# A four-layer decoder trunk on one core: who makes the remainders of layer 2's weights

## The chip, the cores and the metric

One core of one Trainium2 chip runs the whole program in one launch. The metric is the device time of an execution in microseconds; lower is better. The engines are TensorE (PE, matmuls), VectorE (DVE), ScalarE (ACT), GpSimd (POOL) and SyncE (SP, which issues DMAs). Their instruction streams run side by side and meet only at semaphores.

## The reference, cut to what matters

The input is x of 256 tokens by 2048 features in float32. Four pre-norm residual layers follow, whose mixers are differential attention, sliding-window attention with sinks, mLSTM, and differential attention again, and a final RMSNorm. Layer 2, the one that the change touches, is the sliding-window layer:

```python
proj = h @ w_in                     # h: 256 x 2048, w_in: 2048 x 4608
q, k, v, g = jnp.split(proj, [SW_WIDTH, SW_WIDTH + nkv, SW_WIDTH + 2 * nkv], axis=-1)
q = rope(q.reshape(B, S, SW_Q_HEADS, d), cos, sin) * (d ** -0.5)
...
o = o.reshape(B, S, SW_WIDTH) * jax.nn.silu(g.astype(jnp.float32))
return o.astype(h.dtype) @ w_out    # w_out: 2048 x 2048
```

It has 32 query heads and 4 key/value heads of width 64.

## The kernel before, in words

**Three products for one.** Each float32 operand of a projection is split in two: a rounded part ("hi") and the remainder ("lo"). A product is then the sum of three matmuls: hi by hi, lo of the activations by hi of the weights, hi of the activations by lo of the weights (`three`, lines 1134 to 1138). The weights are split while they stream in.

**Jobs and pairs.** A projection is cut into jobs of 512 output columns. A job has 2048 rows of weights, 16 chunks of 128, worked in 8 pairs of chunks. A pair is a tile of 128 partitions by 1024 columns (512 KB). For each pair:

- SP loads `raw` (8 pairs of room, lines 640 to 653), when the pair eight before is done;
- ACT rounds it into `w_hi` (a ring of 4 pairs, lines 1065 to 1074) after waiting for the load and for the pair four before to be done, and raises `hi_ready`;
- DVE subtracts, `w_lo = raw - w_hi` (8 pairs of room, lines 2008 to 2016), after waiting for `hi_ready`, and raises `lo_ready`;
- PE waits for `lo_ready` (line 1317), makes 12 matmuls of 512 columns (2 chunks, 2 halves of the tokens, 3 products) and raises `pairs_done`.

There are 73 jobs, so 584 pairs. Layer 2 has one head job (keys and values), then four iterations of two jobs (512 columns of queries, 512 columns of the gate), then four jobs of the output projection. One iteration is thus 16 pairs, numbered 0 to 15 below, and serves 8 query heads.

**Side work.** Everything that isn't a projection is hung on pairs. `walk` (line 273) calls the function `pair` of every engine for the same pairs in the same order, and each of them first or last calls the layer's side function. A table written out by hand (`SW`, line 70) says at which pair each step is due; steps with a number of 16 or more fall in the next iteration. In layer 2, on DVE ahead of a pair's subtraction: the rope of the queries at pairs 11 and 12 (lines 1560 to 1565), sums of attention outputs (line 1727), the gating of the iteration before (line 1792), its split (line 1796, at pairs 13 and 14), the staging of the values (line 1744, at pair 15), and the lower half of the split of the queries (line 1759, from pair 15). On PE behind a pair's matmuls: the transposes of the queries at pair 11 (line 1102), and the scores of one head after each of the pairs 12 to 15 and the following four (lines 1209 to 1211). The scores of the first head wait for `split_lo`, which line 1759's first instruction raises; those of the second for the bank that its second instruction frees.

**GpSimd** does small things only: constants at the start, and the inverse roots of the norms (lines 724 to 731), three instructions on a handful of columns each time. In layer 2 it makes the layer's norm and then goes straight on to wait for the next layer's (line 742).

Of the kernel before, what the change touches and what calls it, by code (L numbers as in the profile page):

```python
# [22 lines left out]
F32 = mybir.dt.float32  # L23
F32R = mybir.dt.float32r
I32 = mybir.dt.int32
ALU = mybir.AluOpType
# [8 lines left out]
PAIRS = KC // 2  # L35
RING = 8
LAG = 4
ITERS = 4
# [5 lines left out]
LAYERS = [("da", 0), ("sw", 0), ("ml", 0), ("da", 1)]  # L44
NL = len(LAYERS)
HEAD_JOBS = {"da": 0, "sw": 1, "ml": 0}
ITER_JOBS = {"da": 4, "sw": 2, "ml": 4}
# [115 lines left out]
def in_iter(l, name, i, n):  # L163
    head, per, _ = _counts(l, name)
    return i * per + (BASE[name][l] + head + n)
# [7 lines left out]
def _jobs():  # L173

    first, loop, out, by = [], [], [], []
    for kind, _ in LAYERS:
        first.append(len(by))
        by += ["act"] * HEAD_JOBS[kind]
        loop.append(len(by))

        by += ITER_EMPTIED_BY[kind] * ITERS
        out.append(len(by))
        by += ["dve"] * OUT_JOBS
    return first, loop, out, by


JOB0, LOOP0, OUT0, EMPTIED_BY = _jobs()
# [82 lines left out]
        return (l, places.index(at)) if at in places else None  # L270


def walk(eng, l, pair, own=None, who=None):

    kind = LAYERS[l][0]
    nj = ITER_JOBS[kind]
    for p in range(PAIRS * HEAD_JOBS[kind]):
        pair(Place(l, "head", None, p), JOB0[l], 0, 0, p)
    for j in range(nj):
        for p in range(PAIRS):  # L280
            pair(Place(l, "iter", 0, j * PAIRS + p), LOOP0[l] + j, 0, j, p)
    with eng.Fori(1, ITERS) as i:
        if own:
            own.enter(i, OWN_STEPS[who, kind])
        for j in range(nj):
            for p in range(PAIRS):
                pair(Place(l, "iter", i, j * PAIRS + p), LOOP0[l] + j, i, j, p)
        if own:
            own.leave()
    for j in range(OUT_JOBS):  # L290
        for p in range(PAIRS):
            pair(Place(l, "out", None, j * PAIRS + p), OUT0[l] + j, 0, j, p)


def build(nc, x, positions, norm_g, final_g, da_w_in, da_w_out, da_lambda, da_subln_g, sw_w_in, sw_w_out,
          sw_sinks, ml_w_in, ml_b_gates, ml_w_out, ml_norm_g, freqs, out):
    ctx = ExitStack()
    with ctx:
        def sb(name, shape, dt=F32):
            return ctx.enter_context(nc.sbuf_tensor(name, shape, dt))  # L300

        def sem(name):
            return ctx.enter_context(nc.semaphore(name))
# [6 lines left out]
        with ExitStack() as place:  # L310
            raw = place.enter_context(nc.sbuf_tensor("raw", [P, KC, JW], F32))
        w_lo = sb("w_lo", [P, KC, JW], F32R)
        w_hi = sb("w_hi", [P, RING, JW], F32R)
# [172 lines left out]
        raw_full = [sem(f"raw_full{s}") for s in range(PAIRS)]  # L486
        raw_half = [sem(f"raw_half{s}") for s in range(PAIRS)]
        hi_ready, lo_ready = sem("hi_ready"), sem("lo_ready")
        first_in, first_hi, first_lo = sem("first_in"), sem("first_hi"), sem("first_lo")
        pairs_done = sem("pairs_done")  # L490
        act_emptied, dve_emptied = sem("act_emptied"), sem("dve_emptied")
# [205 lines left out]
        @block.gpsimd  # L697
        def _(pool):
            own = Own(pool, pool_own)

            def select(ap, compare, fill, base, step, channel):
                pool.affine_select(out=ap, in_=ap, compare_op=compare, fill=fill, base=base,
                                   pattern=[[step, P]], channel_multiplier=channel).then_inc(consts, 1)

            own.step(pool.memset(ident[:], 0.0))
            own.wait()
            select(ident[:], ALU.not_equal, 1.0, 0, -1, 1)
            for t in (masks, mask_ml, x_ss):
                own.step(pool.memset(t[:], 0.0))
            for t in (ones, tri):  # L710
                own.step(pool.memset(t[:], 1.0))
            own.step(pool.memset(half_pow[:], -0.5))
            own.step(pool.memset(eps_t[:], EPS))
            for width, t in inv_width.items():
                own.step(pool.memset(t[:], 1.0 / width))
            own.wait()

            for c in (1, 3):
                select(masks[:, P * c:P * c + P], ALU.is_ge, NEG, 0, -1, 1)
            select(masks[:, 2 * P:3 * P], ALU.is_gt, NEG, 0, 1, -1)  # L720
            select(mask_ml[:], ALU.is_ge, -NEG, 0, 1, -1)
            select(tri[:], ALU.is_ge, 0.0, 0, 1, -1)

            def inverse_root(to, ms, ss, width):

                n = ms.shape[1]
                own.step(pool.tensor_tensor(ms, ss, inv_width[width][:, 0:n], ALU.mult))  # L727
                own.wait()
                own.step(pool.tensor_tensor(ms, ms, eps_t[:, 0:n], ALU.add))
                own.wait()  # L730
                return pool.tensor_tensor(to, ms, half_pow[:, 0:n], ALU.pow)

            for l in range(NL):
                pool.wait_ge(x_summed, l + 1)
                inverse_root(rstd[:], x_ms[:], x_sum[:], D).then_inc(rstd_ready, 1)
                pool.wait_ge(rstd_ready, 2 * l + 1)
                pool.tensor_scalar(rstd_half[:], rstd[:], 0.5, 0.0, ALU.mult, ALU.add).then_inc(rstd_ready, 1)
                if l == 0:
                    wg_rows = ml_w_in[0, :, 3 * D:3 * D + 16].rearrange("(k p) n -> p k n", p=P)
                    pool.dma_start(wg_raw[:], wg_rows).then_inc(wg_in, 16)  # L740
                if LAYERS[l][0] == "sw":
                    continue
                kind = LAYERS[l][0]
                with pool.Fori(0, ITERS) as i:
                    own.more = i * OWN_STEPS["pool", kind]
                    if kind == "da":
                        for h in range(2):
                            pool.wait_ge(sig["ssq_done"], in_iter(l, "ssq_done", i, 2 * h + 2))
                            inverse_root(o_rs[:, h, :], o_ms[:, h, :], o_ss[:, h, :], S).then_inc(sig["o_rstd"], 1)
                    else:  # L750
                        flat = [a[:].rearrange("p a b -> p (a b)") for a in (o_rs, o_ms, o_ss)]
                        pool.wait_ge(sig["ssq_done"], in_iter(l, "ssq_done", i, 4))
                        inverse_root(*flat, S).then_inc(sig["o_rstd"], 1)
                own.more = 0
                own.n += (ITERS - 1) * OWN_STEPS["pool", kind]
            for t in range(T):
                pool.wait_ge(x_summed, NL + t + 1)
                pool.tensor_tensor(rstd[:, t:t + 1], x_ms[:, t:t + 1], half_pow[:, 0:1], ALU.pow).then_inc(rstd_ready, 1)
# [335 lines left out]
        def _(pe):  # L1094
# [216 lines left out]
            def pair(w, j0, i, j, p):  # L1311
                J = j0 + ITER_JOBS[w.kind] * i
                w.first_job_of_layer = j0 == JOB0[w.l] and (w.phase == "head" or w.first)
                if w.start and w.idx == 0:
                    pe.wait_ge(first_lo, 1)
                else:
                    pe.wait_ge(lo_ready, PAIRS * J + p + 1)
                slot, whole = 2 * (p % LAG), 2 * p
                if w.phase == "out":
                    j, p = OUT[w.kind]["order"][w.idx]  # L1320
                    j0 = OUT0[w.l] + j
# [45 lines left out]
                if w.start and w.idx in (0, 1, 3):  # L1367
                    n = {0: 1, 1: 2, 3: 3}[w.idx]
# [18 lines left out]
        def _(dve):  # L1387
# [605 lines left out]
            def pair(w, j0, i, j, p):  # L1993
                J = j0 + ITER_JOBS[w.kind] * i
                if (ln := w.x_due("sum")) is not None:
                    add_residual(*ln)
                if (ln := w.x_due("total")) is not None:
                    sum_squares(ln[0])
                if (ln := w.x_due("split")) is not None:
                    x_turned_lo(*ln)  # L2000
                if (ln := w.x_due("gain")) is not None and ln[0] == NL - 1:
                    final_gain(ln[1])
                sides[w.kind](w, w.l)
                if w.start and w.idx == 0:
                    dve.wait_ge(first_hi, 1)
                    dve.tensor_tensor(w_lo[:, 0, :], raw[:, 0, :], w_hi[:, 0, :].bitcast(F32), ALU.subtract)\
                       .then_inc(first_lo, 1)
                dve.wait_ge(hi_ready, PAIRS * J + p + 1)
                q = 2 * (p % LAG)
                if w.start and w.idx == 0:  # L2010
                    dve.tensor_tensor(w_lo[:, 1, :], raw[:, 1, :], w_hi[:, 1, :].bitcast(F32), ALU.subtract)\
                       .then_inc(lo_ready, 1)
                else:
                    two = slice(2 * p, 2 * p + 2)
                    dve.tensor_tensor(w_lo[:, two, :], raw[:, two, :], w_hi[:, q:q + 2, :].bitcast(F32),  # L2015
                                      ALU.subtract).then_inc(lo_ready, 1)
                if w.start:
                    start_up(w.idx)

# [3 lines left out]
            last = OUT_JOBS - 1  # L2023
# [62 lines left out]
```

## Time and profile before

| what | value |
| --- | --- |
| median of 3 runs | 1712.66 us (1712.31 to 1713.44) |
| the profiled execution's own time | 1712.57 us |
| its span, from the first to the last instruction | 1710.8 us |
| granted TensorE clock over the span | 0.999 of full speed |
| busy: PE, DVE, ACT, POOL | 1699.6, 1188.9, 911.4, 38.9 us |
| HBM traffic | 213 GB/s over the span |
| share of PE in the chain that ended last | 95% |

Busy times count an engine's own instructions, not its waits, branches or the issuing of DMAs. Ends of matmuls are modelled and matmuls overlap, so PE's lines are best read by their starts. A line's busy time is followed by the mean of one instruction in ns. Times in rows of a timeline are from the start of the span.

### The profile page before, as it was taken

What the parts mean: (1) busy time and instruction counts of PE and PEld (TensorE: products, weight loads), DVE (VectorE), ACT (ScalarE), POOL (GpSimd) and SP (SyncE); (2) the same over time, 40 slices, a digit from 0 to 9 for tenths busy, and PEclk for the clock granted to TensorE, in tenths of its full rate; (3) what the DMA queues carried; (4) which work ended last, traced back from release to release, by engine and by line L of the source; (5) the groups of instructions that cost most, each with busy time, mean ns of one, the idle gap of its engine ahead of it and who ended that gap; (6) DMA issues with size and microseconds to landing.
All of it is one profiled execution on the core that took longest, in us unless ns stands there. A gap on an engine that the chain in (4) does not pass through costs nothing.

```text
span 1710.8 us, 24445 instructions
## 1 busy us (share of the span) xinstructions
PE 1699.6 (99%) x7890; PEld 1417.7 (83%) x7890; DVE 1188.9 (69%) x1909; ACT 911.4 (53%) x1400; POOL 38.9 (2%) x99
## 2 busy tenths in 40 slices
PE   9999999999999999999999999999999999999998
PEld 7888888888888888888888888888888888888887
DVE  7767677775769888865656465656676676777756
ACT  7454555554656666655544545454554555455543
POOL 1000000000000000000000000000000000000000
PEclk9999999999999999999999999999999999999999
DMA  8768676766875555478998699966877686767673
GB/s 286 244 194 262 201 245 215 233 216 220 264 216 161 160 159 153 154 234 194 190 166 271 177 201 182 265 182 216 260 227 237 195 265 200 247 214 232 223 237 126
DMA packets 230035, 364.53 MB, mean 213 GB/s; under 512 B 14950, under 2 KB 80044, under 8 KB 229836
## 3 DMA queue, kind: packets, MB, share of 16 engines
q1 hardware_dynamic: 229536, 362.94, 73.5%
q8 instruction: 39, 0.64, 0.2%
q0 software_dynamic: 48, 0.13, 0.1%
q10 hardware_dynamic: 380, 0.56, 0.1%
q14 instruction: 32, 0.26, 0.0%
HBM read 335.79 MB, written 27.79 MB: 213 GB/s over the span
## 4 chain that ended last, share of the span: by engine, by line
PE 95%; DMA 2%; issue 1%; SPq 1%; DVE 1%; ACT 0%; DVEq 0%; POOLq 0%; POOL 0%; ACTq 0%
PE acc L1136 29%; PE acc L1137 29%; PE acc L1138 29%; PE tp L1102 1%; PE tp L1137 1%; PE tp L1136 1%; PE tp L1138 1%; DMA raw<-in_ml_w_in_dram 1%; PE sc L1137 1%; PE sc L1136 1%; PE sc L1138 1%; DMA xres<-in_x_dram 0%; DMA qs<-q_turning 0%; DMA q_turning<-scr 0%; PE sc L1162 0%
## 5 line engine op out<-in xcount | busy, mean ns | idle before, releaser
L2015 DVE TENSOR_TENSOR w_lo<-raw,w_hi 128x1024 fp32r<-128x1024 f32 x583 | 703.2, 1220 | 401.4 <-ACT w_hi L1074 399.0
L1074 ACT ACTIVATE w_hi<-raw 128x1024 fp32r<-128x1024 f32 x583 | 610.2, 1056 | 454.9 <-PE acc L1138 401.6
L1136 PE MATMUL acc<-w_hi,xt_hi 128*128 128x512 f32 x1824 | 715.3, 392 | 1.7 <-DVE w_lo L2015 1.0
L1138 PE MATMUL acc<-w_hi,xt_lo 128*128 128x512 f32 x1824 | 711.0, 390 | 0.0
L1137 PE MATMUL acc<-w_lo,xt_hi 128*128 128x512 f32 x1824 | 710.4, 389 | 0.0
L1138 PEld LDWEIGHTS acc<-w_hi,xt_lo 128*128 128x128 f32 x1824 | 342.4, 188 | 72.3
L1136 PEld LDWEIGHTS acc<-w_hi,xt_hi 128*128 128x128 f32 x1824 | 342.6, 188 | 70.3 <-DVE w_lo L2015 1.6
L1137 PEld LDWEIGHTS acc<-w_lo,xt_hi 128*128 128x128 f32 x1824 | 342.6, 188 | 67.3
L1136 PE MATMUL acc<-w_hi,ot_hi 128*128 128x512 f32 (+1 forms) x456 | 176.6, 387 | 0.0
L1138 PE MATMUL acc<-w_hi,ot_lo 128*128 128x512 f32 (+1 forms) x456 | 175.8, 386 | 0.0
L1137 PE MATMUL acc<-w_lo,ot_hi 128*128 128x512 f32 (+1 forms) x456 | 175.8, 385 | 0.0
L877 ACT ACTIVATE scr<-scr,neg_max_t 128x128 f32<-128x128 f32 (+1 forms) x128 | 57.3, 448 | 95.8 <-DVE neg_max_t L1591 75.6
L1138 PEld LDWEIGHTS acc<-w_hi,ot_lo 128*128 128x128 f32 x456 | 85.7, 188 | 17.2
L1136 PEld LDWEIGHTS acc<-w_hi,ot_hi 128*128 128x128 f32 x456 | 85.7, 188 | 16.8
L1137 PEld LDWEIGHTS acc<-w_lo,ot_hi 128*128 128x128 f32 x456 | 85.7, 188 | 16.7
L805 ACT ACTIVATE junk_x<-xres 128x512 f32<-128x512 f32 x38 | 24.0, 632 | 40.7 <-DVE xres L1980 40.1
L890 ACT ACTIVATE junk_o<-sc 128x256 f32<-128x256 f32 x32 | 12.3, 384 | 37.4 <-PE sc L1138 36.9
L727 POOL TENSOR_TENSOR o_ms<-o_ss,inv 128x2 f32<-128x2 f32 (+1 forms) x20 | 3.9, 197 | 1059.4 <-ACT junk_o L890 1059.4
L863 ACT ACTIVATE th<-acc,rstd_half 128x512 f32<-128x512 f32 x32 | 20.2, 682 | 12.8 <-PE acc L1138 12.8
L845 ACT ACTIVATE qs<-acc,rstd 128x512 f32<-128x512 f32 x32 | 20.3, 684 | 12.3 <-PE acc L1138 12.2
L1636 DVE SCALAR_TENSOR_TENSOR v_lo<-acc,rstd,v_hi 128x512 fp32r<-128x512 f32 x24 | 16.9, 746 | 13.6 <-ACT v_hi L855 13.6
L1136 PE MATMUL tp<-w_hi,ot_hi 128*128 128x512 f32 x64 | 24.9, 389 | 0.0
(306 smaller groups left out, 1226.5 us busy)
## 6 DMA issues: line engine op xcount, KB each, us to landing
raw<-in_da_w_in_dram SPq DMA_DIRECT2D x255, 512.0 KB, 4.4
raw<-in_ml_w_in_dram SPq DMA_DIRECT2D x96, 512.0 KB, 5.7
raw<-in_sw_w_in_dram SPq DMA_DIRECT2D x72, 512.0 KB, 3.7
raw<-in_da_w_out_dram SPq DMA_DIRECT2D x64, 512.0 KB, 4.0
raw<-in_sw_w_out_dram SPq DMA_DIRECT2D x32, 512.0 KB, 3.7
raw<-in_ml_w_in_dram SPq DMA_DIRECT2D x64, 256.0 KB, 7.3
raw<-in_ml_w_out_dram SPq DMA_DIRECT2D x32, 512.0 KB, 3.9
qs<-q_turning SPq DMA_DIRECT2D x12, 512.0 KB, 6.9
```

The costliest lines, as they stand in the source:

```text
L805: act.activation(junk_x[:], xres[:, t, JW * n:JW * n + JW], ACT.Square, accum_out=x_ss[:, t, n:n + 1]).then_inc(sig["x_sq"], 1)
L845: act.activation(dst[:, t], src, ACT.Copy, scale=rstd[:, t:t + 1]).then_inc(act_emptied, 1)
L863: act.activation(dst[:, t, :], acc[b][t][:], ACT.Tanh, scale=rstd_half[:, t:t + 1])\
L877: act.activation(scr[:, slot, cols], scr[:, slot, cols], ACT.Exp, bias=neg_max_t[:, slot, t:t + 1], scale=scale, accum_out=exp_sum[:, slot ...
L890: act.activation(junk_o[:], ml_values(h, t)[:, 0:S] if ml else sc[h][:, S * t:S * t + S], ACT.Square, scale=1.0 if scale is None else scal ...
L1074: act.activation(w_hi[:, q:q + 2, :], raw[:, 2 * p:2 * p + 2, :], ACT.Copy).then_inc(hi_ready, 1)
L1102: m = pe.transpose(dst, src, ident[0:n, 0:n])
L1136: pe.matmul(out_ap, k_hi, m_hi, start=start, stop=False)
L1137: pe.matmul(out_ap, k_hi, m_lo, start=False, stop=False)
L1138: return pe.matmul(out_ap, k_lo, m_hi, start=False, stop=stop)
L1636: dve.scalar_tensor_tensor(lo[:, t], src, rstd[:, t:t + 1], hi[:, t].bitcast(F32), ALU.mult, ALU.subtract)\
L2015: dve.tensor_tensor(w_lo[:, two, :], raw[:, two, :], w_hi[:, q:q + 2, :].bitcast(F32), ALU.subtract).then_inc(lo_ready, 1)
```

## The change

In the four iterations of layer 2 the subtraction of every odd pair of a job (p = 1, 3, 5, 7) is left out on DVE and made by GpSimd. GpSimd waits for the same `hi_ready` and raises a semaphore of its own, `lo_pool`; PE waits for `lo_pool` at these pairs, and for `lo_ready` at the others, whose counts are lowered by the pairs that GpSimd has taken. DVE still waits for `hi_ready` at every pair. The head job and the output projection of layer 2, and the other layers, stay as they are but for the counts.

```diff
+POOL_PAIRS = PAIRS // 2
+
+
+def pool_makes_lo(w, p):
+
+    return w.kind == "sw" and w.phase == "iter" and p % 2 == 1
+
+
+def made_by_pool(w, j, p):
+
+    if w.kind == "sw" and w.phase == "iter":
+        return POOL_PAIRS * j + p // 2
+    last = max((n for n in range(NL) if LAYERS[n][0] == "sw"))
+    return POOL_PAIRS * ITER_JOBS["sw"] * ITERS if w.l > last or w.l == last and w.phase == "out" else 0
...
+            def rest(J, p):
+
+                two, q = slice(2 * p, 2 * p + 2), 2 * (p % LAG)
+                pool.wait_ge(hi_ready, PAIRS * J + p + 1)
+                pool.tensor_tensor(w_lo[:, two, :], raw[:, two, :], w_hi[:, q:q + 2, :].bitcast(F32), ALU.subtract)\
+                    .then_inc(lo_pool, 1)
+
...
                 if LAYERS[l][0] == "sw":
+                    for j in range(ITER_JOBS["sw"]):
+                        for p in range(1, PAIRS, 2):
+                            rest(LOOP0[l] + j, p)
+                    with pool.Fori(1, ITERS) as i:
+                        for j in range(ITER_JOBS["sw"]):
+                            for p in range(1, PAIRS, 2):
+                                rest(LOOP0[l] + ITER_JOBS["sw"] * i + j, p)
                     continue
...
                 if w.start and w.idx == 0:
                     pe.wait_ge(first_lo, 1)
+                elif pool_makes_lo(w, p):
+                    pe.wait_ge(lo_pool, i * (POOL_PAIRS * ITER_JOBS["sw"]) + (POOL_PAIRS * j + p // 2 + 1))
+                elif w.kind == "sw" and w.phase == "iter":
+                    per = (PAIRS - POOL_PAIRS) * ITER_JOBS["sw"]
+                    pe.wait_ge(lo_ready, i * per + (PAIRS * j0 + p + 1 - made_by_pool(w, j, p)))
                 else:
-                    pe.wait_ge(lo_ready, PAIRS * J + p + 1)
+                    pe.wait_ge(lo_ready, PAIRS * J + p + 1 - made_by_pool(w, j, p))
...
                     two = slice(2 * p, 2 * p + 2)
-                    dve.tensor_tensor(w_lo[:, two, :], raw[:, two, :], w_hi[:, q:q + 2, :].bitcast(F32),
-                                      ALU.subtract).then_inc(lo_ready, 1)
+                    if not pool_makes_lo(w, p):
+                        dve.tensor_tensor(w_lo[:, two, :], raw[:, two, :], w_hi[:, q:q + 2, :].bitcast(F32),
+                                          ALU.subtract).then_inc(lo_ready, 1)
```

## Rows read from the trace of the kernel before

**Rows 1.** The page, part 1: busy us, share of the span, instructions.
```profile
PE 1699.6 (99%) x7890; PEld 1417.7 (83%) x7890; DVE 1188.9 (69%) x1909; ACT 911.4 (53%) x1400; POOL 38.9 (2%) x99
```

**Rows 2.** The waits of PE: us in total, times, longest us.
```profile
PE sc L1125 <- POOL ident L702: 1.6, 1, 1.6
PE acc L1136 <- DVE w_lo L2015: 1.0, 2, 0.6
```

**Rows 3.** Windows: PE, PEld, DVE, ACT, POOL busy us; PEclk, DMA share, GB/s.
```profile
574.00:628.00 54.00, 54.00 (x274) 45.55 (x272) 47.37 (x113) 36.52 (x74) 0.00 (x0) 1.00 0.55 155
```

**Rows 4.** Timeline of PE, layer 2: start us, us, what it is.
```profile
571.37 0.39 PE L1136 MATMUL acc<-w_hi,xt_hi 128*128 128x512 f32 x1
...
577.73 0.28 PE L1209 MATMUL sc<-k_all,q_split 128*128 x1
...
578.09 0.39 PE L1136 MATMUL acc<-w_hi,xt_hi 128*128 128x512 f32 x1
...
631.74 0.28 PE L1209 MATMUL sc<-k_all,q_split 128*128 x1
```

**Rows 5.** The page, part 5: line 2015 over the whole run.
```profile
L2015 DVE TENSOR_TENSOR w_lo<-raw,w_hi 128x1024 fp32r<-128x1024 f32 x583 | 703.2, 1220 | 401.4 <-ACT w_hi L1074 399.0
```

**Rows 6.** Groups of POOL by line: busy us, mean ns, idle before.
```profile
L727 POOL TENSOR_TENSOR o_ms<-o_ss,inv 128x2 f32<-128x2 f32 (+1 forms) x20 | 3.9, 197 | 1059.4 <-ACT junk_o L890 1059.4
...
L702 POOL TENSOR_SCALAR_AFFINE_SELECT masks<-masks 128x128 f32<-128x128 f32 x3 | 0.8, 291 | 0.1
L709 POOL MEMSET masks<- 128x512 f32 x1 | 0.5, 523 | 0.0
...
L709 POOL MEMSET mask_ml<- 128x128 f32 x1 | 0.2, 203 | 0.0
```

**Rows 7.** Timeline of DVE, second iteration of layer 2, pairs 11 to 15.
```profile
564.75 0.69 DVE L1560 TENSOR_TENSOR shared<-qs,cos_b 128x512 f32<-128x512 f32 x1 [3.02 <-ACT qs L845]
...
566.76 1.22 DVE L2015 TENSOR_TENSOR w_lo<-raw,w_hi 128x1024 fp32r<-128x1024 f32 x1
...
570.79 0.68 DVE L1792 TENSOR_TENSOR th<-tp,th 128x512 f32<-128x512 f32 x1
571.39 1.22 DVE L2015 TENSOR_TENSOR w_lo<-raw,w_hi 128x1024 fp32r<-128x1024 f32 x1
572.52 0.68 DVE L1796 TENSOR_TENSOR ot_lo<-th,ot_hi 128x512 f32 x1
573.23 1.23 DVE L2015 TENSOR_TENSOR w_lo<-raw,w_hi 128x1024 fp32r<-128x1024 f32 x1
...
574.98 1.22 DVE L2015 TENSOR_TENSOR w_lo<-raw,w_hi 128x1024 fp32r<-128x1024 f32 x1
576.11 0.29 DVE L1744 TENSOR_TENSOR v_hi<-shared,v_hi 128x128 fp32r<-128x128 f32 x1
576.43 1.41 DVE L1759 TENSOR_TENSOR q_split<-tp,q_split 64x512 fp32r<-64x512 f32 x2
```

**Rows 8.** Timeline of ACT, the same pairs.
```profile
562.28 1.06 ACT L1074 ACTIVATE w_hi<-raw 128x1024 fp32r<-128x1024 f32 x1 [1.38 <-PE acc L1138]
...
572.15 2.00 ACT L1074 ACTIVATE w_hi<-raw 128x1024 fp32r<-128x1024 f32 x2
...
574.29 1.06 ACT L1074 ACTIVATE w_hi<-raw 128x1024 fp32r<-128x1024 f32 x1
575.38 1.21 ACT L953 ACTIVATE q_split<-tp 64x512 fp32r<-64x512 f32 x2
```

**Rows 9.** Timelines of DVE and POOL where the two overlap, in two places.
```profile
472.34 1.22 DVE L2015 TENSOR_TENSOR w_lo<-raw,w_hi 128x1024 fp32r<-128x1024 f32 x1
...
472.50 1.11 POOL L727 TENSOR_TENSOR x_ms<-x_sum,inv 128x2 f32<-128x2 f32 x1 [72.82 <-DVE x_sum L1544]
...
1358.62 0.69 POOL L731 TENSOR_TENSOR o_rs<-o_ms,half_pow 128x2 f32<-128x2 f32 x1
...
1358.97 1.23 DVE L2015 TENSOR_TENSOR w_lo<-raw,w_hi 128x1024 fp32r<-128x1024 f32 x1 [3.50 <-ACT w_hi L1074]
```

More of the change, by code:

```diff
@@ L488, in build @@
         hi_ready, lo_ready = sem("hi_ready"), sem("lo_ready")
+        lo_pool = sem("lo_pool")
         first_in, first_hi, first_lo = sem("first_in"), sem("first_hi"), sem("first_lo")
```

## The prediction

> **What bounds the kernel now.** First the page's list of busy times: TensorE (PE) is busy 1699.6 of the 1710.8 us span, VectorE (DVE) 1188.9, GpSimd (POOL) 38.9 [rows 1]. Then the waits of TensorE over the run: the largest is 1.6 us, for a constant at the start, and for line 2015's product it waits 1.0 us in all [rows 2]. Then the table by stretches of 54 us, which is one iteration of layer 2: in it PE is busy 54.00 of 54.00 us at the full granted clock (2.4 GHz), DVE 47.4, ScalarE 36.5, POOL 0 [rows 3]. The first score matmul of the second iteration starts at 577.73 us and that of the third at 631.74, 54.01 us later [rows 4]. So layer 2 is TensorE's own work from end to end; no wait of PE is there to be removed. DVE is the second busiest, at 88%, and has lead enough that none of its lateness reaches PE.
>
> The profiled execution took 1712.57 us (span 1710.8 and 1.8 around it), 0.09 below the median of the runs, 1712.66. I count against the first and give the sum on the second, which shifts nothing. A difference under 0.2% (3.4 us) counts as none.
>
> **The change part by part.**
>
> Removed from DVE: 4 iterations by 2 jobs by 4 odd pairs = 32 subtractions of 1.22 us (line 2015 [rows 5]) = 39 us of DVE time, 9.8 us in each 54 us. It is worth nothing to the end by itself, as PE waits for no DVE instruction there. DVE still waits for the rounded half (hi_ready) of each odd pair, so its side work runs no further ahead than now; only its backlogs shrink.
>
> Added to POOL: 32 subtractions of 128x1024. No such instruction stands in the trace. The nearest rows: a memset takes 203 ns for 128 columns and 523 for 512 [rows 6], so 0.83 ns per column written and 0.1 us fixed; an affine select that also reads 128 columns takes 291, so 0.69 ns per column read. One write and two reads: 0.10 + 1024 x (0.83 + 2 x 0.69) = 2.36 us. Lower end: all streams run beside one another, 0.95 us. Upper end: each of three costs what a write costs and the subtraction as much again, 3.5 us. I take 2.36; POOL is then busy 32 x 2.36 = 76 us of 216, so its throughput is no question, and its own queue holds nothing else until the next layer's norm.
>
> Counts on PE: each wait is one wait as before, on another semaphore. A semaphore read costs nothing visible. DMA queues, ACT's order and the tiles' reuse are untouched: raw is reloaded after pairs_done, and w_lo of a pair is overwritten only after hi_ready of eight pairs later.
>
> What decides is lateness at one place, pairs 11 to 15 of each iteration. Take the second iteration [rows 7, 8]. ACT ends w_hi of pair 11 at 563.34, of pairs 13 and 14 (the two in a row) at 573.2 and 574.15, of pair 15 at 575.35. PE starts pair 13 at 578.09 [rows 4], so POOL has 4.89 us for it: 2.36 leaves 2.5. Pair 11 is used at 571.37, over five us after POOL would be done. Elsewhere ACT makes w_hi as soon as the pair four before is done (line 1069), three pairs ahead: 3 x 12 matmuls x 0.23 us, less its own 1.06, leaves 7 us, so the other odd pairs are safe. Without interference the POOL pairs are in time, and with the upper end of 3.5 us too.
>
> The tighter partner is DVE's split of the queries (line 1759), whose first half ends at 577.12, 0.61 us before the score matmul at 577.73 that waits for it. In front of it on DVE's queue stand w_lo of pair 13 (573.23, removed), line 1796, w_lo of pair 14 (574.98), line 1744. With pair 13 gone, pair 14's can start when its w_hi has landed, at 574.2, and the split when ACT has its half (575.38 + 0.60), at 576.0 instead of 576.43: 0.4 us more lead. Also worth nothing.
>
> Interference is the unknown. POOL's multiply of 128x2 takes 0.20 us as a rule [rows 6], but 1.11 when DVE's line 2015 was running: it began at 472.50 and ended at 473.61, 0.05 after DVE's did at 473.56 [rows 9]. So POOL waits while DVE reads two SBUF tiles. The other way round, DVE's 2015 began 0.35 us into a POOL power of 0.69 us and took its usual 1.23 [rows 9]: no hold shows, though two columns are soon read, so this says little of 1024.
>
> If only POOL yields: its pair 13 runs from 573.25, DVE's two-input work in that time is line 1796 (0.68), w_lo of pair 14 (1.22) and line 1744 (0.29): 573.25 + 2.36 + 2.2 = 577.8, 0.3 us before PE wants it. The term is 0, and up to 0.3 us per iteration with a slightly longer instruction.
>
> By the Trainium skill ("SBUF — State Buffer", Who interferes with whom) it is a lock for both: a DVE instruction with two SBUF inputs contends with a GpSimd one that reads SBUF, and "the other **fully blocks**" until the first is finished. That rule speaks against the change; by it the sum would not be 0 but one of the first two rivals below. The rows agree for POOL behind DVE (1.11 against 0.20) and show nothing for DVE behind POOL.
>
> Sum: 0 (removed) + 0 to 1.2 (pair 13 in four iterations) = about 1712.7 to 1713.9.
>
> **Rivals.**
>
> *DVE is held too, but keeps its turn while its instructions follow without a gap.* POOL's pair 11 (563.4 to 565.8) holds the rope from 564.75 by 1.0 us, the removed w_lo of 566.76 gives 1.2 back, so line 1792 stays at about 570.8. Line 1796 ends at 573.8, POOL's pair 13 runs to 576.2, pair 14's w_lo to 577.4, line 1744 to 577.7, the split to 578.4: PE waits 0.7 us, in the three iterations that have a predecessor's tail: +2.1 us, 1714.8. For it: DVE's starts overlap the ends before (571.39 + 1.22 against 572.52). It still lies within 0.2%.
>
> *Slower: DVE is held and POOL is let in between two of its instructions.* Then POOL's pair 15, ready at 575.35, goes in front of line 1744: 577.4 to 579.8, line 1744 to 580.1, split to 580.8; PE stands 3.05 us at the score. Three times 9.2, and 0 to 3 in the first iteration, whose DVE work has another order: +9 to +12, some 1723. It decides once the delay per iteration passes 0.85 us (3.4 us / 4). For it: 32 instructions twice as long as DVE's, at the place where DVE's lead is 0.6 us. Against: a 12% idle DVE, given 9.8 us back in every iteration, and rows 9, where DVE is never held.
>
> *Slower: the instruction is longer than my upper end,* 4.5 us or more, by a slower path for this type or by many small holds. Pair 13 is then late by the excess over 4.8 us, and POOL holds DVE for longer: +1 to +3 per iteration, 1717 to 1725.
>
> *Faster* needs a PE wait that the trace does not have. *Nothing is done* (POOL takes no work) cannot be, since PE waits for POOL's own semaphore.
>
> **How the numbers follow.** Hidden or nearly so (0 to +1.2): 0.41. Held with DVE keeping its turn (+1 to +3): 0.18. POOL let in between (+9 to +12): 0.24. Long instruction (+4 to +12): 0.14. Faster: 0.03. Same is 0.41 + 0.18 = 0.59 and slower 0.38. The likeliest, the first, gives 1713.2; its own range is 1712.2 to 1714.5, with the second to 1715.5. As the slower cases hold 0.38, the range has to reach over them: 1712.2 to 1724.
>
> **What would show it.** Right: the first score matmuls of the iterations still 54.0 us apart and PE busy 54.00 of 54.00; POOL's line near 2.4 us by 32; line 2015 at 551 instructions of 1.22; no wait of PE for w_lo or q_split. DVE held: line 2015 or 1560 with a mean over 1.3 us in layer 2. POOL let in: line 1744 or 1759 a POOL instruction late, and a wait of PE of 2 to 3 us at line 1209. Long instruction: a wait at line 1136 for POOL's w_lo, at pair 13. Wrong altogether: any stretch of layer 2 shorter than before, or a wait in another layer.

## The result and the profile after

The changed kernel takes 1738.47 us (median, 1737.12 to 1740.0), against 1712.49 for the kernel before in the same runs: a ratio of 1.0151, 95% interval 1.0139 to 1.0163. It is 26 us slower. The forecast of 1713.2 and its range up to 1724.0 both miss.

| what | before | after |
| --- | --- | --- |
| span of the profiled execution | 1710.8 us | 1738.0 us |
| granted TensorE clock over the span | 0.999 | 0.995 |
| busy: PE, DVE, POOL | 1699.6, 1188.9, 38.9 | 1709.6, 1202.8, 116.9 |

The first lines of the page answer to rows 1 and 5. DVE was given 39 us less to do and is busy 14 us longer. The time that an instruction stands still is part of its own duration here, so it counts as busy and no view of waits lists it; "held" below means an instruction that is recorded as longer than others of its kind.

```profile
PE 1709.6 (98%) x7890; PEld 1421.4 (82%) x7890; DVE 1202.8 (69%) x1877; ACT 909.3 (52%) x1400; POOL 116.9 (7%) x131
...
L2052 DVE TENSOR_TENSOR w_lo<-raw,w_hi 128x1024 fp32r<-128x1024 f32 x551 | 672.8, 1235 | 395.1 <-ACT w_hi L1105 392.7
...
L754 POOL TENSOR_TENSOR w_lo<-raw,w_hi 128x1024 fp32r<-128x1024 f32 x32 | 78.2, 2445 | 154.7 <-ACT w_hi L1105 154.7
```

Some lines have moved: 2015 is 2052 now, 1593 (the negated row maximum) is 1629, 1744 is 1780, 1759 is 1795, 1796 is 1832, 1191 to 1194 (attention times values) are 1222 to 1225, 1209 is 1240. In the experiments they move by a few more. The waits of PE over the whole run (us in total, times, longest), the answer to rows 2:

```profile
PE sc L1240 <- DVE q_split L1795: 7.8, 3, 2.6
PE sc L1222 <- DVE th L1763: 3.6, 3, 1.2
PE sc L1222 <- issue: 3.6, 3, 1.2
PE sc L1240 <- issue: 2.1, 1, 2.1
```

None of them is for GpSimd's product. PE waits for the split of the queries at the first score of three iterations. The fourth wait there, put down to "issue", is that of the first iteration, and it is the same one: the split's first half (526.18, 0.69 us) ends 0.1 us before the matmul at 526.97. Twice in each of three tails (the part of an iteration's attention that falls in the next one) PE waits at line 1222; three of these six waits are put down to DVE, the others to "issue". The first scores, the answer to rows 4 (PE's timeline):

```profile
588.61 0.38 PE L1240 MATMUL sc<-k_all,q_split 128*128 x1 [2.61 <-DVE q_split L1795]
...
650.28 0.38 PE L1240 MATMUL sc<-k_all,q_split 128*128 x1 [2.61 <-DVE q_split L1795]
```

They are 61.67 us apart where they were 54.01, so an iteration loses 7.66. Each matmul's start set against the same one's before says where its lateness grows: 2.8 us at the first score (2.3 in the first iteration), then 1.6 over the following pair, 1.4 to 1.5 at each of two attention matmuls (line 1222) and 0.3 at the transposes behind them. Four times the head (4.4, and 3.9 in the first iteration) and three times the tail (3.2) make 26.8 of the 27.2 us between the spans.

**Why the split is late.** DVE's timeline in the second iteration, pairs 12 to 15, the answer to rows 7, and GpSimd's:

```profile
580.40 0.69 DVE L1832 TENSOR_TENSOR ot_lo<-th,ot_hi 128x512 f32 x1
581.33 2.78 DVE L1832 TENSOR_TENSOR ot_lo<-th,ot_hi 128x512 f32 x1 [0.24 <-ACT w_hi L1105]
584.04 3.41 DVE L2052 TENSOR_TENSOR w_lo<-raw,w_hi 128x1024 fp32r<-128x1024 f32 x1
587.37 0.28 DVE L1780 TENSOR_TENSOR v_hi<-shared,v_hi 128x128 fp32r<-128x128 f32 x1
587.68 1.41 DVE L1795 TENSOR_TENSOR q_split<-tp,q_split 64x512 fp32r<-64x512 f32 x2
```

```profile
581.16 2.40 POOL L754 TENSOR_TENSOR w_lo<-raw,w_hi 128x1024 fp32r<-128x1024 f32 x1 [7.25 <-ACT w_hi L1105]
...
583.55 2.82 POOL L754 TENSOR_TENSOR w_lo<-raw,w_hi 128x1024 fp32r<-128x1024 f32 x1
```

The two instructions of line 1832 are alike; the first takes 0.69 us, the second, begun 0.17 after GpSimd's pair 13, takes 2.78 and ends at 584.11, 0.55 after GpSimd does: it stood still for 2.1 us, though no semaphore stands between the two engines there. So the engines' streams don't meet only at semaphores, as the text ahead of the prediction has it. Then GpSimd's pair 15, begun at 583.55, has to wait for that end (2.82 instead of 2.40), and is let in ahead of DVE's pair 14, which begins at 584.04 and ends at 587.45, 1.08 after GpSimd's 586.37. So each waits for the end of the other's instruction, and they take turns. The split comes at 587.68 instead of 576.43. PE was already 8.1 us late by then, so the split is 3.2 us late against it, with a lead of 0.6.

**Why the following pair is slow.** By the table by stretches (columns as in rows 3), PE's granted clock is 0.50 from 590 to 592, that is 1.2 instead of 2.4 GHz, behind a stop in which no matmul was begun between 585.61 and 588.61. The matmuls are 0.43 us apart there instead of 0.23. That the stop is what lowers the clock is tested in experiment 9.

```profile
588.00:589.00 1.00, 0.39 (x3) 0.40 (x4) 0.97 (x2) 0.32 (x1) 0.00 (x0) 1.00 0.90 342
589.00:590.00 1.00, 1.00 (x6) 0.78 (x6) 0.71 (x5) 0.00 (x0) 0.00 (x0) 0.72 0.29 109
590.00:592.00 2.00, 2.00 (x6) 1.63 (x5) 1.85 (x7) 0.99 (x4) 0.00 (x0) 0.50 0.00 0
```

**Why the tail is late.** The row maximum's small instruction, 128x2, which reads one tile and a column of scalars, took 228 to 231 ns in all 32 cases before. Here, with GpSimd at work since 609.45 for 2.39 us, it takes 2.20 and ends with it (GpSimd's and DVE's timelines, then ACT's and PE's):

```profile
609.45 2.39 POOL L754 TENSOR_TENSOR w_lo<-raw,w_hi 128x1024 fp32r<-128x1024 f32 x1 [5.51 <-ACT w_hi L1105]
...
609.67 2.20 DVE L1629 TENSOR_SCALAR neg_max_t<-row_max,sink_cur 128x2 f32<-128x2 f32 x1
613.54 0.87 DVE L1763 TENSOR_TENSOR th<-sc,o_rest 64x256 f32<-64x256 f32 x2 [1.67 <-ACT o_rest L1012]
...
614.97 0.56 DVE L1843 TENSOR_TENSOR v_lo<-tp,v_hi 128x384 fp32r<-128x384 f32 x1
```

```profile
611.90 0.40 ACT L908 ACTIVATE scr<-scr,neg_max_t 128x128 f32<-128x128 f32 x1 [2.15 <-DVE neg_max_t L1629]
...
612.91 0.59 ACT L1012 ACTIVATE o_rest<-sc 64x512 f32<-64x512 f32 x1
...
615.73 0.49 PE L1222 MATMUL sc<-v_hi 128*128 128x512 f32 x1 [1.19 <-issue]
```

ACT's exponential waits for it, behind that the evacuation at 612.91, for which DVE's line 1763 waits. Behind that, on DVE's queue, line 1843 ends at 615.53; it frees the bank that PE's attention matmul waits for in the kernel's code, and that matmul starts at 615.73. A chain through three engines hangs on an instruction of 0.23 us.

### The profile page after: what moved, and what is told of

It reads as the page before. It is cut to its first block, busy times and chain, and to the rows that moved or that the text cites. A ratio compares the mean times of both kernels' runs of the same rounds, so it can differ in the third digit from the quotient of the medians.

```text
span 1738.0 us, 24486 instructions
## 1 busy us (share of the span) xinstructions
PE 1709.6 (98%) x7890; PEld 1421.4 (82%) x7890; DVE 1202.8 (69%) x1877; ACT 909.3 (52%) x1400; POOL 116.9 (7%) x131
## 4 chain that ended last, share of the span: by engine, by line
PE 55%; DMA 2%; issue 1%; DVE 1%; SPq 0%; ACT 0%; POOLq 0%; DVEq 0%; POOL 0%; ACTq 0%
PE acc L1167 17%; PE acc L1168 17%; PE acc L1169 17%; DMA raw<-in_ml_w_in_dram 1%; PE tp L1167 1%; PE tp L1169 1%; PE tp L1168 1%; DMA qs<-q_turning 0%; PE sc L1168 0%; PE sc L1167 0%; DMA q_turning<-scr 0%; PE sc L1169 0%; PE tp L1133 0%; SPq L583 0%; PE sc L1193 0%
## 5 line engine op out<-in xcount | busy, mean ns | idle before, releaser
L2052 DVE TENSOR_TENSOR w_lo<-raw,w_hi 128x1024 fp32r<-128x1024 f32 x551 | 672.8, 1235 | 395.1 <-ACT w_hi L1105 392.7
L754 POOL TENSOR_TENSOR w_lo<-raw,w_hi 128x1024 fp32r<-128x1024 f32 x32 | 78.2, 2445 | 154.7 <-ACT w_hi L1105 154.7
L1629 DVE TENSOR_SCALAR neg_max_t<-row_max,sink_cur 128x2 f32<-128x2 f32 x32 | 28.3, 885 | 3.6
```

The source lines that it names most:

```text
L754: pool.tensor_tensor(w_lo[:, two, :], raw[:, two, :], w_hi[:, q:q + 2, :].bitcast(F32), ALU.subtract)\
L1629: op = dve.tensor_scalar(neg_max_t[:, slot, :], row_max[:, slot, :], -(64 ** -0.5), sink_cur[:, slot:slot + 1], ALU.mult, ALU.min)
```

## The experiments

Theory A is this reading: instructions of GpSimd and VectorE that overlap hold each other, and the holds reach PE. Theory B puts the loss on GpSimd's product and its semaphore, theory C on the shifted order of DVE's queue. Times are medians; the kernel before took 1713.35 us beside the first four, 1713.6 beside the next four, 1713.86 beside the last three. Ratios are to it.

### 1. The relief alone

```diff
-                    pe.wait_ge(lo_pool, i * (POOL_PAIRS * ITER_JOBS["sw"]) + (POOL_PAIRS * j + p // 2 + 1))
+                    pe.wait_ge(hi_ready, PAIRS * J + p + 1)
...
-                    return three(banks[t][:], hi[:, k, c], lo[:, k, c], w_hi[:, at, :], w_lo[:, at_lo, :], k == 0, stop)
+                    rest = w_hi[:, at, :] if pool_makes_lo(w, p) else w_lo[:, at_lo, :]
+                    return three(banks[t][:], hi[:, k, c], lo[:, k, c], w_hi[:, at, :], rest, k == 0, stop)
```

and GpSimd's loops in layer 2 are taken out. The odd pairs' remainder is thus left out of the product.

> The odd pairs' subtraction is left out everywhere: neither VectorE nor GpSimd makes it, and TensorE reads the rounded half in its place (same matmuls, same count), waiting for hi_ready. Theory A (VectorE is held by GpSimd's instructions, whichever way they meet): no GpSimd work, so no loss, 1712.5 us within 1.5. Theory B (GpSimd's product or its semaphore comes late to TensorE): also 1712.5. Theory C (taking the instructions out of VectorE's queue shifts its order against ScalarE's and that costs): about 1738.

Measured: 1713.12 us, ratio 0.9995 (0.9986 to 1.0005). Taking 39 us from DVE neither gains nor costs. Theory C falls, and the prediction's first term, nothing for the relief, stands.

### 2. and 3. GpSimd at work for nobody: two reads, or none

DVE makes every remainder again, PE waits for both semaphores, and `rest` on GpSimd is one of these (its loop over iterations unrolled):

```diff
-                pool.tensor_tensor(w_lo[:, two, :], raw[:, two, :], w_hi[:, q:q + 2, :].bitcast(F32), ALU.subtract)\
-                    .then_inc(lo_pool, 1)
+                for c in range(2):      # g_two
+                    own.step(pool.tensor_tensor(junk_x[:], w_hi[:, q + c, :].bitcast(F32), w_hi[:, q + c, :].bitcast(F32), ALU.subtract))
+                    own.wait()
+                pool.sem_inc(lo_pool)
...
+                for c in range(4):      # g_set
+                    own.step(pool.memset(junk_x[:], 0.0))
+                    own.wait()
+                pool.sem_inc(lo_pool)
```

> VectorE makes every subtraction as before; GpSimd makes two useless 128x512 subtractions of w_hi from itself at the odd pairs (same 2.4 us, two reads and a write), and TensorE also waits for GpSimd's semaphore. Theory A: VectorE has 39 us more work than in the changed kernel and is held as often, so the loss is at least half of the changed kernel's and perhaps more, 1728 to 1765, and VectorE's instructions with two SBUF reads show means well over their usual ones. Theory B: the loss is that of the changed kernel, 1738, with TensorE waiting for lo_pool. Theory C: 1712.5, since VectorE's queue is that of before.

> As the run before it, but GpSimd's useless work is four memsets of 128x512 (about 2.1 us, writes and no reads). Theory A, in the form that it is the reading of SBUF that holds VectorE: 1712.5 to 1714, and VectorE's lines have their usual durations. Theory A in a wider form (any GpSimd instruction holds): as the run before. Theory B: as the run before, since times and semaphores are alike.

Measured: with the subtractions 1730.68 us, ratio 1.0090 (1.0072 to 1.0108); with the memsets 1713.56, ratio 0.9997 (0.9988 to 1.0007). The semaphores, the waits and 67.5 us of memsets on GpSimd (128 of them) cost nothing, so theory B falls; the subtractions, 87.3 us of GpSimd with their holds, cost 17 us. They differ from the memsets in reading and in length (1.04 us against 0.53 when not held); experiment 10 takes these apart. The expected size, at least half of 26, is met. It isn't more than the changed kernel's, though DVE has 39 us more to do; each of the two instructions is less than half as long as the changed kernel's one. Groups of DVE from 575 to 730 us, with subtractions and then with memsets:

```profile
L2051 DVE TENSOR_TENSOR w_lo<-raw,w_hi 128x1024 fp32r<-128x1024 f32 x44 | 57.3, 1302 | 0.2
...
L1629 DVE TENSOR_SCALAR neg_max_t<-row_max,sink_cur 128x2 f32<-128x2 f32 x24 | 9.5, 397 | 2.7
```

```profile
L2051 DVE TENSOR_TENSOR w_lo<-raw,w_hi 128x1024 fp32r<-128x1024 f32 x48 | 58.6, 1220 | 1.8 <-ACT w_hi L1107 1.6
...
L1629 DVE TENSOR_SCALAR neg_max_t<-row_max,sink_cur 128x2 f32<-128x2 f32 x24 | 6.6, 273 | 2.7
```

The memsets leave the subtraction at 1220 ns but not the row maximum: the mean is 273 against 229, and the longest takes 629, 0.4 us more than usual and so less than the whole of one memset (527 ns). One COPY of 128x8 into `sink_cur` is held by the memsets too, 602 ns.

### 4. and 5. Shorter instructions on GpSimd

```diff
+                for c in (2 * p, 2 * p + 1):      # half: two of 128x512
+                    m = pool.tensor_tensor(w_lo[:, c, :], raw[:, c, :], w_hi[:, q + c % 2, :].bitcast(F32), ALU.subtract)
+                m.then_inc(lo_pool, 1)
```

`quarter` cuts each of them once more, to four of 128x256.

> The changed kernel with GpSimd's subtraction cut in two instructions of 128x512; the product is ready at the same time. Theory A: a hold lasts at most half as long (1.2 us instead of 2.4), so the wait at the first score falls from 2.8 to about 1.5 us, the half-clock stretch behind it goes, and the two waits of 1.5 us in the tail go down to 0.3: 1717 to 1726. If VectorE is let in only behind both halves, 1738. Theory B: 1738.

> GpSimd's subtraction in four instructions of 128x256. Theory A with a hold that ends with each instruction: a VectorE instruction is held 0.7 us at most each time, the stop at the first score shrinks from 1.9 us (halves) to about 1, with no half-clock stretch: 1714.5 to 1718. If VectorE has to wait again at every quarter, no better than halves, 1722.

Measured: halves 1722.37 us, ratio 1.0042 (1.0028 to 1.0056), quarters 1714.26, ratio 1.0006 (0.9996 to 1.0015), though GpSimd is busier with them (101.4 us for 128 instructions). These two and the changed kernel differ in nothing but the length of GpSimd's instructions. DVE is let in between the pieces, so one hold lasts one piece. Halves fall in the expected range, quarters 0.2 us below theirs. DVE's timeline with halves, over the stretch shown above:

```profile
577.52 1.67 DVE L1833 TENSOR_TENSOR ot_lo<-th,ot_hi 128x512 f32 x1 [0.24 <-ACT w_hi L1106]
579.12 2.32 DVE L2053 TENSOR_TENSOR w_lo<-raw,w_hi 128x1024 fp32r<-128x1024 f32 x1
581.36 1.37 DVE L1781 TENSOR_TENSOR v_hi<-shared,v_hi 128x128 fp32r<-128x128 f32 x1
582.75 1.41 DVE L1796 TENSOR_TENSOR q_split<-tp,q_split 64x512 fp32r<-64x512 f32 x2
```

Three DVE instructions are held in a row, each for 1.0 to 1.1 us. The tail's waits are gone. The stops at the first score make PE 2.3 us later in the first iteration and 1.8 in each of the others. Only the first is followed by the half clock (0.50 from 527.8 to 530.4, 1.7 us lost); behind the second the clock is 1.00. With quarters PE becomes 0.5 us later at the first of these places and 0.15 to 0.17 at the others.

### 6. Is it the second operand of the row maximum?

```diff
-                    op = dve.tensor_scalar(neg_max_t[:, slot, :], row_max[:, slot, :], -(64 ** -0.5),
-                                           sink_cur[:, slot:slot + 1], ALU.mult, ALU.min)
+                    op = dve.tensor_scalar(neg_max_t[:, slot, :], row_max[:, slot, :], -(64 ** -0.5), None, ALU.mult)
```

> The changed kernel, with the small instruction that makes the negated row maximum (128x2) given a constant instead of its second operand from SBUF (the minimum with the sinks is left out of the shift). Theory A1 (what holds a VectorE instruction is a second operand read from SBUF, a column of scalars too): this line goes back to 0.23 us, the two tail waits of 1.5 us per iteration go, 9 to 10 us less than the changed kernel: 1728. Theory A2 (this kind of instruction is held whatever its second operand, since the memsets held it a little too, 273 ns against 229, and not the subtraction): the line keeps its mean of 0.9 us and the time is 1738.

Measured: 1739.25 us, ratio 1.0150 (1.0133 to 1.0167): A2. With one tile read and nothing else the instruction is held as before, 169 ns at the least and 2251 at the most. It is the kind of instruction, not the second operand.

```profile
L1629 DVE TENSOR_SCALAR neg_max_t<-row_max x32: 169/170/2251, 527.5 to 737.5; 128x2 f32<-128x2 f32 x32
```

### 7. and 8. The two halves of the loss apart

`POOL_IDX` names the pairs of an iteration that GpSimd makes, and the counts follow it:

```diff
-    return w.kind == "sw" and w.phase == "iter" and p % 2 == 1
+    return w.kind == "sw" and w.phase == "iter" and w.idx in POOL_IDX
```

It is (1, 3, 5, 7, 9) in the first of these two kernels, `tail`, and (11, 13, 15) in the second, `hot`.

> GpSimd makes only pairs 1, 3, 5, 7 and 9 of an iteration, VectorE the others. Theory A, with the loss located by the trace: the stop at the first score (2.8 us and 1.6 us of half clock in each of four iterations) goes, the two waits in the tail (3.3 us in three iterations) stay: 1720 to 1723. If the two parts are not independent (a late tail helps or hurts the head of the next iteration), further off than that.

> The complement: GpSimd makes only pairs 11, 13 and 15. Theory A: the stops at the first score stay with their half-clock stretches, the tail waits go: 1728 to 1731. The two losses (this one and that of the complement) add up to the changed kernel's 26 us.

Measured: 1723.17 us, ratio 1.0059 (1.0042 to 1.0076), and 1729.74, ratio 1.0097 (1.0080 to 1.0114). By the ratios 10 and 17 us, together 27 against the 26 of the change; the first is 0.2 us above its expected range, the second inside. In the trace of `hot` PE's stops are as long as the changed kernel's, but what the clock adds behind them is not the same each time: 0, 1.6, 1.4 and 2.9 us (see the last section). The waits of PE are those of the one place or the other:

```profile
PE sc L1222 <- issue: 3.9, 3, 1.4
PE sc L1222 <- DVE th L1763: 3.6, 3, 1.2
```

```profile
PE sc L1240 <- DVE q_split L1795: 7.8, 3, 2.6
PE sc L1240 <- issue: 2.1, 1, 2.1
```

### 9. The clock

```diff
                         if h == 0:
                             pe.wait_ge(free["sc_1"], in_head(l, "sc_1", 1))
+                            fill_wait("sc_0", in_iter(l, "sc_0", i, 0))
+                            for _ in range(10):
+                                pe.matmul(sc[0][:], xt_hi[:, 0, 0:P], xt_hi[:, 0:2, :].rearrange("p a n -> p (a n)"),
+                                          start=True, stop=True)
```

> The changed kernel, with ten useless matmuls of 512 columns (2.3 us at full clock) put on TensorE in front of the first score of each iteration, where it stands still for 2.4 to 2.8 us. Theory A: they fit into the stop and cost nothing, and if the half-clock stretch behind the stop comes from TensorE having been idle, it goes: 4 times 1.6 us less, 1738 - 6 = 1731 to 1733. Rival: the clock falls for another reason, or the matmuls run at half clock themselves: 1738 or more.

Measured: 1732.87 us, ratio 1.0113 (1.0096 to 1.0130). Forty more matmuls, and 5.6 us less than without them by the medians, 6.5 by the ratios; four times 1.6 is 6.4. PE becomes 2.3 and 2.7 us later at the first scores, no more than in the changed kernel, so the matmuls themselves cost nothing. Behind all four stops the granted clock is 1.00, and the four runs lie within 1732.8 to 1733.7 us, where those of the changed kernel go from 1737.1 to 1740.0. The ten run 0.24 us apart inside the stop, and the pair behind it keeps its 0.23 us:

```profile
582.92 2.43 PE L1234 MATMUL sc<-xt_hi 128*128 128x512 f32 x10
585.63 0.38 PE L1244 MATMUL sc<-k_all,q_split 128*128 x1 [0.28 <-DVE q_split L1799]
...
586.78 0.39 PE L1167 MATMUL acc<-w_hi,xt_hi 128*128 128x512 f32 x1
587.00 0.39 PE L1168 MATMUL acc<-w_lo,xt_hi 128*128 128x512 f32 x1
```

### 10. One read instead of two

As experiment 2, with four copies `pool.tensor_copy(junk_x[:], w_hi[:, q + c, :].bitcast(F32))` for each odd pair.

> VectorE makes every subtraction; GpSimd makes four useless copies of 128x512 from w_hi at the odd pairs: one read and one write each. Theory A with any read of SBUF by GpSimd as what holds two-input instructions: line 2015's mean in layer 2 rises over 1.25 us (memsets left it at 1.22) and the time over 1714; each hold lasts one copy, so 1714 to 1722. Rival: only GpSimd's instructions with two inputs hold: 1.22 us and 1713.5.

Measured: 1721.42 us, ratio 1.0043 (1.0027 to 1.0060), in the expected range. A copy takes 0.62 us when not held, little more than a memset (0.53), and there are four of each, so it is the read and not the length that separates 8 us from nothing. One read is enough to hold DVE's two-input instructions; in the stretch from 575 to 730 us:

```profile
L2051 DVE TENSOR_TENSOR w_lo<-raw,w_hi 128x1024 fp32r<-128x1024 f32 x46 | 59.2, 1288 | 0.2
```

Set beside the quarters, this run says that the length of a hold is not all. Its pieces are shorter (0.62 us against 0.74) and it loses 8 us where they lose nothing that the medians show. Here DVE still makes the odd pairs' remainders, pair 13's among them, in front of the split (DVE's timeline, second iteration):

```profile
577.81 1.23 DVE L2051 TENSOR_TENSOR w_lo<-raw,w_hi 128x1024 fp32r<-128x1024 f32 x1
578.96 1.10 DVE L1832 TENSOR_TENSOR ot_lo<-th,ot_hi 128x512 f32 x1
579.98 1.63 DVE L2051 TENSOR_TENSOR w_lo<-raw,w_hi 128x1024 fp32r<-128x1024 f32 x1
581.53 0.69 DVE L1780 TENSOR_TENSOR v_hi<-shared,v_hi 128x128 fp32r<-128x128 f32 x1
582.25 1.41 DVE L1795 TENSOR_TENSOR q_split<-tp,q_split 64x512 fp32r<-64x512 f32 x2
```

PE becomes 1.7 us later there, against 0.15 with quarters. Experiment 2 has the same sign: pieces of 1.04 us cost 17 us, halves of 1.30 cost 9. So the relief of DVE, worth nothing alone, covers part of the holds. This is read from timelines; these kernels differ in what GpSimd reads and writes too, and no two runs with the same work on GpSimd differ in the relief alone.

### 11. Only where there is lead

`POOL_IDX` is (1, 3, 9).

> GpSimd makes only pairs 1, 3 and 9 of an iteration. In the changed kernel's trace the two tail waits go back to holds of the row maximum's line by pairs 5 and 7, and the stop at the score to pairs 13 and 15. Theory A (a hold costs only where it lies on a chain with too little lead): no loss, 1712.5 to 1714.5, though VectorE is held 12 times. Rival (lateness adds up over all holds, whichever they are): half of the tail's loss, 1717 to 1719.

Measured: 1713.06 us, ratio 0.9998 (0.9989 to 1.0008). GpSimd makes 12 of the 64 remainders and holds the row maximum's line up to 2252 ns, and nothing reaches PE; lateness doesn't simply add up over holds:

```profile
L1629 DVE TENSOR_SCALAR neg_max_t<-row_max,sink_cur x32: 227/229/2252, 525.6 to 712.6; 128x2 f32<-128x2 f32 x32
```

No version beats the kernel before. The relief alone, the memsets, the quarters and this one equal it within their intervals, and rows 3 say why none is faster: PE has nothing idle in layer 2.

## Why the prediction was wrong, by its steps

- **Nothing to gain.** Right: PE's 54.00 of 54.00 us [rows 3], and experiment 1.
- **GpSimd's price.** Estimated 2.36 us from a memset and an affine select [rows 6]; 2.40 measured where it is not held (78.2 us in all, against 76 forecast). The sum is right partly by luck: by the same working a copy of 128x512 would take 0.10 + 512 x (0.83 + 0.69) = 0.88 us, and experiment 10 has 0.62. That the product would be in time was right too: no wait of PE is for it.
- **The place.** Right in the head of an iteration: the split of the queries, which had 0.6 us of lead, became PE's stop.
- **The step that failed** is "If only POOL yields ... The term is 0", taken as the likeliest case. It rested on rows 9, where a DVE instruction ran its usual 1.23 us behind a GpSimd instruction over two columns; the prediction itself said that this tells little of 1024 columns, and still gave the case 0.41. What the Trainium skill states ("SBUF — State Buffer", Who interferes with whom), that the one that begins second stands still to the end of the first, is what the trace shows for both sides, with 2.78 against 0.69 us for DVE and 2.82 against 2.40 for GpSimd. The hold of DVE by GpSimd, put at nothing, was up to 2.2 us for one instruction and, with what followed from it, 7.66 us an iteration.
- **The rival that came true** is the second (DVE held, GpSimd let in between two DVE instructions; chance 0.24). Its term for the head was 3.05 us an iteration, 2.8 was measured (2.3 in the first, where it had 0 to 3), 10.6 us in all. The turns came in another order: GpSimd's pair 13 went ahead of line 1796's second instruction, and its pair 15 ahead of DVE's pair 14 and not only of line 1744. Either way both GpSimd instructions stand before the split, so the sum is the same. But +9 to +12 is less than half of 26, since two terms were missing. The half clock behind each stop cost 1.6 us, some 6.5 in all: the prediction saw a stop of 3 us coming and priced the stop only. And the tail cost 3.2 us in each of three iterations, some 10 in all: the prediction looked for instructions with two SBUF tiles and took "the other odd pairs are safe" from GpSimd's own lead. It had not looked at what else DVE would be doing during GpSimd's other five instructions, and it doesn't name the row maximum's line. An instruction of 0.23 us can be held as long as a long one.
- **The range** reached 1724.0 because the second rival was priced too low; its point of decision, 0.85 us an iteration, was passed by far (7.66).

## What to carry to other kernels

Work moved from VectorE to GpSimd does not simply run beside VectorE's: where VectorE's instruction is of a kind that is held, the two take turns, one whole instruction at a time. So list the VectorE instructions that can fall into a GpSimd instruction and are of such a kind (here those with two SBUF inputs, and tensor-scalar ones over SBUF however small), price each as late by the whole of it, then follow who waits. Cut GpSimd's instructions short (32 of 2.4 us cost 26 us, the same work in 128 pieces of 0.74 us nothing that the medians show), or let it work only where the lead is longer. Short pieces alone are no guarantee: 128 copies of 0.62 us cost 8 us where VectorE kept all its own work. And where TensorE had no idle time, relief of another engine gained nothing, so any such risk is taken for no gain.

## What the runs showed of the hardware that had not been expected

- A VectorE tensor-scalar instruction over 128x2 with one SBUF input is held too, by GpSimd's subtractions (up to 2251 ns instead of 169, in experiment 6) and by its memsets (up to 629 instead of 228, with a column of scalars as second operand), while the memsets leave the two-input subtraction at 1220 ns. The same section of the Trainium skill counts this kind of instruction among those that can take both shared ports, and tensor-tensor ones as sharing only the read side; the runs agree with both. That it is the ports is the page's account, and these runs show only who holds whom.
- Not every VectorE instruction is held. Line 1613, which reads its scores from PSUM, takes its usual 0.42 us at 557.33, inside a subtraction of GpSimd (557.01 to 559.40), while the row maximum right behind it, at 558.08, takes 1.35 and ends with GpSimd's.
- GpSimd is let in between two VectorE instructions even where these follow each other without a gap, once it has been waiting: pair 15's ends at 586.37, between VectorE's ends at 584.11 and 587.45.
- The same stop of TensorE was sometimes followed by the lower clock and sometimes not. In the changed kernel all four stops were: eight matmuls 0.43 us apart, 1.6 us lost each time. In `hot`, PE becomes 2.3 us late at its first stop and the clock stays at 1.00; at its fourth it becomes 2.8 us late and the clock is 0.50 for 5.5 us, 2.9 us lost (table by stretches, columns as in rows 3):

```profile
525.50:528.50 3.00, 3.00 (x15) 2.57 (x16) 2.76 (x8) 1.17 (x5) 0.00 (x0) 1.00 0.36 139
698.80:704.30 5.50, 5.49 (x14) 4.44 (x15) 3.38 (x9) 0.99 (x4) 0.00 (x0) 0.50 0.07 25
```

The first stops of experiments 6 (2.3 us) and 10 (2.5) and the last of experiment 2 (2.4) were not followed by it either, the first of the halves (2.3) was, and no stop that made PE 1.8 us late or less was. What decides it these runs don't show, so a stop's price by the clock is an average and not a constant.
